# Last group of the third expert stage: which weights lie outside the ring of slots, an up matrix loaded in halves, and the order of two roots in the closing norm

## What is computed

```
def _hier_moe(h, wg, bg, we, be, w_gate, w_up, w_down):    # h (256, 1024)
    g_sel = argmax(h @ wg + bg)                            # 1 of 4 groups
    top_v, top_i = top_k(e_logits of that group, 2)        # 2 of its 8 experts
    ...
    y = (silu(x @ w_gate[e]) * (x @ w_up[e])) @ w_down[e]  # 1024 -> 512 -> 1024
    return sum over the two experts of weight * y

h = h + moe(_rmsnorm(h, norm2_w))
return _rmsnorm(h, final_norm_w)                           # the closing norm
```

## Time and profile before

| | |
|---|---|
| time, median of 3 runs | 1181.17 us (1181.11 to 1182.44) |
| the profiled execution | 1182.97 us, its span 1181.2 us |
| TensorE busy | 1083.0 us (92%) |
| VectorE, ScalarE busy | 333.1 us (28%), 227.3 us (19%) |
| DMA | 364.10 MB, mean 308 GB/s |
| the chain that ended last | TensorE 65%, DMA 27%, VectorE 4% |

### The profile page before, as it was taken

One profiled execution on the slowest core, in us unless ns is written; L12 is line 12 of the kernel. 1 busy time (PEld: TensorE's weight loads), 2 busy tenths in 40 slices (PEclk: granted clock), 3 DMA queues, 4 the chain that ended last, 5 costly groups with the idle time before them and its releaser, 6 DMA issues.

```text
span 1181.2 us, 15578 instructions
## 1 busy us (share of the span) xinstructions
PE 1083.0 (92%) x6382; PEld 539.8 (46%) x6382; DVE 333.1 (28%) x995; ACT 227.3 (19%) x517; POOL 1.0 (0%) x6
## 2 busy tenths in 40 slices
PE   9999999999999999999999989987877887779895
PEld 5555455554787545554465545422421242224231
DVE  1576463113013446111422656100100010001002
ACT  2145341111024423111122232100100010001001
POOL 0000000000000000000000000000000000000000
PEclk9999999999999999999999999999998998999998
DMA  9886368999433148999553248999999999999994
GB/s 318 182 228 242 131 226 358 422 417 379 147 131 143 72 174 319 421 422 341 183 193 143 80 178 322 411 427 428 429 426 428 428 428 427 428 429 428 426 417 197
DMA packets 82820, 364.10 MB, mean 308 GB/s; under 512 B 22690, under 2 KB 28100, under 8 KB 59076
## 3 DMA queue, kind: packets, MB, share of 16 engines
q1 hardware_dynamic: 81956, 363.04, 78.0%
q10 hardware_dynamic: 800, 0.17, 0.1%
HBM read 362.14 MB, written 1.05 MB: 307 GB/s over the span
## 4 chain that ended last, share of the span: by engine, by line
PE 65%; DMA 27%; DVE 4%; ACT 1%; issue 1%; SPq 1%; DVEq 0%
DMA weights<-in_expert_w_down_dram 16%; PE bank L1361 11%; PE bank L926 8%; PE bank L948 7%; DMA weights<-in_expert_w_up_dram 6%; PE bank L1463 5%; PE bank L1420 4%; PE bank L913 4%; DMA weights<-in_moe_w_up_dram 3%; PE bank L938 2%; PE bank L1405 2%; PE bank L1558 2%; PE bank L901 2%; DMA weights<-in_expert_w_gate_dram 2%; PE bank L890 2%; PE bank L1303 1%
## 5 line engine op out<-in xcount | busy, mean ns | idle before, releaser
L1361 PE MATMUL bank<-weights,projected 128*32 128x512 f32 (+1 forms) x1536 | 295.5, 540 | 38.4 <-DMA weights<-in_expert_w_gate_dram 23.7
L1361 PEld LDWEIGHTS bank<-weights,projected 128*32 128x32 f32 (+1 forms) x1536 | 101.9, 121 | 218.2 <-issue 171.4
L926 PE MATMUL bank<-weights,x_transposed 128*128 128x512 f32 x256 | 117.2, 600 | 0.0
L948 PE MATMUL bank<-weights,mixed 128*128 128x512 f32 x192 | 89.7, 604 | 1.6 <-DVE mixed L2578 1.0
L1420 PE MATMUL bank<-weights,work 128*32 128x512 f32 x432 | 53.1, 625 | 22.5 <-DMA weights<-in_expert_w_down_dram 18.0
L926 PEld LDWEIGHTS bank<-weights,x_transposed 128*128 128x128 f32 x256 | 46.4, 191 | 49.3 <-issue 48.4
L1463 PE MATMUL bank<-weights,projected 128*32 128x256 f32 x1024 | 62.2, 396 | 4.5 <-DMA weights<-in_moe_w_up_dram 4.5
L2080 ACT ACTIVATE work<-bank 128x512 f32<-128x512 f32 (+1 forms) x32 | 19.0, 594 | 223.2 <-PE bank L1420 183.2
L2845 DVE TENSOR_TENSOR work<-work,bank 64x512 f32<-64x512 f32 (+1 forms) x22 | 15.0, 682 | 161.3 <-PE bank L1361 159.6
L1558 PE MATMUL bank<-work,heads_transposed 128*128 128x512 f32 x120 | 55.8, 605 | 4.2 <-ACT work L2080 4.2
L2753 DVE COPY work<-bank 64x512 f32<-64x512 f32 (+1 forms) x30 | 20.7, 690 | 113.6 <-PE bank L1420 71.7
(11 more groups left out here) (380 smaller groups left out, 1167.4 us busy)
## 6 DMA issues: line engine op xcount, KB each, us to landing
weights<-in_expert_w_gate_dram SPq DMA_DIRECT2D x30, 2048.0 KB, 17.3
weights<-in_expert_w_up_dram SPq DMA_DIRECT2D x30, 2048.0 KB, 19.5
weights<-in_expert_w_down_dram SPq DMA_DIRECT2D x22, 2048.0 KB, 20.6
weights<-in_moe_w_gate_dram SPq DMA_DIRECT2D x16, 2048.0 KB, 13.0
weights<-in_moe_w_up_dram SPq DMA_DIRECT2D x16, 2048.0 KB, 15.6
weights<-in_moe_w_down_dram SPq DMA_DIRECT2D x12, 2048.0 KB, 13.5
weights<-in_sb_w_in_dram SPq DMA_DIRECT2D x6, 2048.0 KB, 14.6
weights<-in_w_in_dram SPq DMA_DIRECT2D x6, 2048.0 KB, 11.8
```

The lines of the kernel that those rows point to most:

```text
L926: i = mm(BANK[6 + t][:, :], XT[:, kt, t * P:(t + 1) * P], w[:, kt, :], start=kt == 0, stop=kt == KT - 1)
L948: i = mm(BANK[bank][:, :], mixT[:, kt, t * P:(t + 1) * P], w[:, kt, :], start=kt == 0, stop=kt == KT - 1)
L1361: i = mm(b[n_slots * c:n_slots * (c + 1), e * F:(e + 1) * F], x[:, kt, q * n_slots:(q + 1) * n_slots], w[c][:, col:col + F], start=kt == 0 ...
```

## The change

Three things. First, the four outside chunks are now gate0 and up0 of the last group instead of down0 and down1 (`EXTRA_AT = (0, 2)`, `EXTRA_KINDS`); `hidden` reads them with `extra_weights`, and down0 and down1 become ordinary ring blocks. The ring loads of the last group are now: gate1, up1, down0, gate2, up2, down1, gate3, up3, half of down2, down3. Second, up3 is loaded as two halves of both chunks (`load_last_up`), and TensorE begins on it when the first halves are there. Third, in the closing norm ScalarE takes tile 0's root before the two squares of tile 1, and VectorE works out tile 1's mean square between the two halves of tile 0's scaling.

```diff
-EXTRA_AT = (8, 14)
+EXTRA_AT = (0, 2)
+EXTRA_KINDS = ("gate", "up")
...
+                def load_last_up(j):
+                    for h in range(2):
+                        for c in range(2):
+                            n = chunk_no(L, j + c, True)
+                            cols = slice(h * (SLOT // 2), (h + 1) * (SLOT // 2))
+                            if h == 0:
+                                sp.wait_ge(chunk_done, (G - 1) * per_group + (n - NSLOT + 1))
+                            sp.dma_start(slot(n)[:, cols], expert_source(L, "up", G * 2 * units - 2 + c)[:, cols]
+                                         ).then_inc(slot_loaded[n % NSLOT] if h else quarters_loaded[0], 16)
...
-                            sp.dma_start(part, expert_source(L, "down", (G - 1) * 2 * units + c)[:, at:at + cols]).then_inc(extra_loaded[c // 2], 16)
+                            sp.dma_start(part, expert_source(L, EXTRA_KINDS[c // 2], (G - 1) * 2 * units + c % 2)[:, at:at + cols]).then_inc(extra_loaded[c // 2], 16)
...
-                        if 2 * (j // 2) not in EXTRA_AT:
+                        if j == first_chunk(units, "up", units - 1):
+                            load_last_up(j)
+                        elif 2 * (j // 2) not in EXTRA_AT and j != first_chunk(units, "up", units - 1) + 1:
...
-                        w = load(kind, u)
+                        outside = extra and u == 0
+                        x0 = 2 * EXTRA_KINDS.index(kind)
+                        in_halves = extra and (kind, u) == ("up", units - 1)
+                        if in_halves:
+                            pe.wait_ge(quarters_loaded[0], 16 * 8)
+                            w = [slot(chunk_no(L, first_chunk(units, kind, u) + c, last)) for c in range(2)]
+                        elif outside:
+                            pe.wait_ge(extra_loaded[x0 // 2], 16 * sum(len(parts) for parts in EXTRA_PARTS[x0:x0 + 2]))
+                        else:
+                            w = load(kind, u)
...
+                                if in_halves and kt == KT // 2:
+                                    load(kind, u)
...
-                                           w[c][:, col:col + F], start=kt == 0, stop=kt == KT - 1)
-                                    if e == per_chunk - 1 and kt == KT - 1:
+                                           extra_weights(x0 + c, kt) if outside else w[c][:, col:col + F], start=kt == 0, stop=kt == KT - 1)
+                                    if outside and kt == KT - 1 and c:
+                                        i.then_inc(extra_psum, 1)
+                                    elif e == per_chunk - 1 and kt == KT - 1 and not outside:
...
             moe(2, 5)
+            rstd_from(6, (0,))
             act.wait_ge(acc_ready, 6)
             for half in range(2):
                 i = ac(YS[:, 0, half, :], BANK[6 + half][:, :], ACT.Square, accum_out=final_ms[:, half:half + 1])
             i.then_inc(square_ready, 1)
-            rstd_from(6)
+            rstd_from(6, (1,))
...
+                        if after_half and cols.start == 0:
+                            after_half()
...
-                if L == 2:
-                    for t in range(T):
-                        norms(t)
+                    def variance_1():
                         dve.wait_ge(square_ready, 1)
+                        link(tt(newton[:, 1:2], final_ms[:, 0:1], final_ms[:, 1:2], ALU.add))
+                        ts(veps[:, 1:2], newton[:, 1:2], 1.0 / D, RMS_EPS, ALU.mult, ALU.add).then_inc(var_ready, 1)
+
+                    norms(0, variance_1)
+                    norms(1)
```

More of the change, by code:

```diff
@@ L1378, in down @@
                     def down(u, a, half):
-                        outside = extra and u < 2
-                        x0 = 2 * u
                         if a == 0 and half == 0:
                             pe.wait_ge(hT_ready, g * units + (unit0 + u + 1))
-                            if outside:
-                                pe.wait_ge(extra_loaded[u], 16 * sum(len(parts) for parts in EXTRA_PARTS[x0:x0 + 2]))
-                            elif extra and u == SLICE_UNIT:
+                            if extra and u == SLICE_UNIT:
                                 pe.wait_ge(slices_loaded, 16 * 4)
@@ L1417, in down @@
                                         col = f * D + hh * CH
-                                        w = (extra_weights(x0 + c, col // CH) if outside else
-                                             slice_weights(c, col // CH) if sliced else slot(n + c)[:, col:col + CH])
+                                        w = slice_weights(c, col // CH) if sliced else slot(n + c)[:, col:col + CH]
                                         i = mm(BANK[2 + hh][r0:r0 + n_slots, :], hT[:, f, n_slots * c:n_slots * (c + 1)], w,
@@ L1423, in down @@
                                         i.then_inc(y_psum, 1)
-                            i.then_inc(extra_psum if outside else chunk_done, 1 if outside else 2)
+                            i.then_inc(chunk_done, 2)
                             return
@@ L2104, in group @@
                     for u in range(units):
-                        act.wait_ge(chunk_done, g * per_group + (chunk_no(L, first_chunk(units, "gate", u), last) + 2))
+                        if last and L == 2 and u == 0:
+                            act.wait_ge(extra_psum, 1)
+                        else:
+                            act.wait_ge(chunk_done, g * per_group + (chunk_no(L, first_chunk(units, "gate", u), last) + 2))
                         if u:
@@ L2743, in outputs @@
                 def outputs(g, pair, last=False, banks=DOWN_BANK):
-                    if L == 2 and last and pair < 2:
-                        dve.wait_ge(extra_psum, pair + 1)
-                    elif pair % (pairs // units) == pairs // units - 1:
+                    if pair % (pairs // units) == pairs // units - 1:
                         dve.wait_ge(chunk_done, g * per_group + (chunk_no(L, first_chunk(units, "down", pair * units // pairs), last) + 2))
@@ L2842, in group @@
                         dve.wait_ge(silu_done, g * units + (unit0 + u + 1))
-                        dve.wait_ge(chunk_done, g * per_group + (chunk_no(L, first_chunk(units, "up", u), last) + 2))
+                        if last and L == 2 and u == 0:
+                            dve.wait_ge(extra_psum, 2)
+                        else:
+                            dve.wait_ge(chunk_done, g * per_group + (chunk_no(L, first_chunk(units, "up", u), last) + 2))
                         tt(HB[0:rows, :], SG[0:rows, :], BANK[1][0:rows, :], ALU.mult).then_inc(h_ready, 1)
@@ L3047, in _ @@
             mixer_residual(2, N_2 + 7, 1.0, 5, "rms", 5)
-            moe(2, 5, lambda t: normalise(6, "rms", X, t, from_psum=True))
+            moe(2, 5, lambda t, after_half=None: normalise(6, "rms", X, t, from_psum=True, after_half=after_half))
 SMALL_TOTAL = 16 * (NMOE * (1 + G + 2) + 4 + 1 + 5)
```

21 lines of the change are left out of this document (10 added, 11 removed).

## The result

The changed kernel is slower: 1187.38 us median of 6 runs (1186.74 to 1188.06), the kernel before in 6 runs 1182.76 us (1181.11 to 1185.62). The ratio is 1.0042, interval 1.0031 to 1.0053: +5.0 us on 1182.76, between +3.7 and +6.3; the two medians are 4.6 us apart. A second set of runs later gave 1.0035 (1.0022 to 1.0049). The three runs that were known ahead of the change had their median at 1181.17; with more runs the kernel before lies at 1182.1 to 1182.8. All ratios compare fast runs alone, which leaves out one execution of the kernel before (1860.9 us), one of the kernel before with its fourth load held (2249.6 us) and one of the version with up0 and down0 outside and two matmuls added (2836.6 us).

What follows compares the result with a forecast made beforehand. The prediction took the weight stream (426 to 429 GB/s) to bound the third stage. Last group +4.5 us and norm -0.6 us made +3.9 on the median of 1181.17: 1185.1 us, range 1183.4 to 1187.2.

Steps and rivals of the forecast that it cites:

- steps 1 to 3: Last group's ring: gate1 frees its slot at 1103.9, the stream runs dry from 1099.4, the fourth place lands 7.4 us late.
- step 1: Last group up to up0's end: nothing moves, the ring's first three places land as before, up0 ends at 1096.82.
- The first chunk's 7.8 us: Fourth ring place, gate2: a 2 MB chunk issued into an idle queue lands 7.8 us later, at 1111.7.
- The 6.8 us: Same chunk by the skill's rule, 2.0 us fixed plus bytes at 436 GB/s: a sum 1.0 us smaller; not adopted.
- The size of the hole: Last group's weight stream: fourth place's chunk 0 lands at 1111.7 instead of 1104.3, 7.4 us late.
- The start-up: Load into an idle queue: 2.9 us, the 7.8 us to landing less 4.9 us for half a block.
- steps 4 and 5: Tail of last group: no second hole, 0.4 us taken back, last quarter lands at 1170.8, down3 ends at 1171.9.
- The norm: Closing norm: sharpening begins 0.95 us earlier, 0.35 us of small steps move between the halves; term -0.6 us.
- Rival D: Tail: the hole plus a lower clock on down3's last quarter and final scatter, up to 1.7 us more, 1186.8; 9%.
- A: Likeliest case, last group: the hole goes through to the end, 1185.1 us, bounds 1183.9 to 1186.7; 76%.
- the group's term: Last group: down3 ends at 1171.9 instead of 1167.44, term +4.5 us.
- Rival B: Last group's ring: no hole if the fourth place is issued by 1096.5; -3.1 us, 1178.1, faster; 7%.

Runs made afterwards that it cites:

- the repeat: The changed kernel, nothing altered, run and profiled once more against the kernel before: ratio 1.0035 (1.0022 to 1.0049).
- up3 whole: The changed kernel with up3 loaded and awaited whole instead of in halves: ratio to the kernel before 1.0038 (1.0026 to 1.0050).
- old norm: The changed kernel with the closing norm of before, both roots behind the squares: ratio to the kernel before 1.0042 (1.0027 to 1.0058).
- held load: The changed kernel with up0 and down0 outside the ring, gate2's load held until gate1 is used: ratio to the kernel before 1.0035.
- two matmuls added: The changed kernel with one matmul added ahead of the wait for down3's last quarter and one before the last scatter: ratio to the kernel before 1.0032.

## Why the prediction came out as it did

The forecast was slower by 3.9 us, at 1185.1 with a range up to 1187.2. The measured median, 1187.38, lies 0.2 us above the range; the difference was +5.0 us (3.7 to 6.3) and +4.1 in the repeat.

- **The ring (steps 1 to 3): right in its order, 2 us off in its times.** The third load at 1075.9, the next 25.8 us later, nothing moved in between, gate1 with no wait. The text had named a gate1 that starts before 1096 as a sign of being wrong, and it started at 1094.59 (1094.0 and 1094.3 in two more profiles): not by another order of work, but since gate0 started about 2 us earlier (1080.1) than in the profile of before (1082.07), so step 1's "nothing moves" doesn't hold from one execution to the next. The first chunk's 7.8 us from the earlier trace rows were 7.7, and 7.7 to 8.0 in the other kernels with a dry queue. The 6.8 us, an estimate by the rule of the Trainium skill ("DMA: Bandwidth & Descriptors", section "Anatomy of one DMA — SWDGE (gpsimd) path"), is not what this queue shows.
- **The size of the hole: 7.4 us forecast, 5.6 on the first chunk and 6.6 on the second and at the end measured.** Two terms were off, in opposite directions. The release came 2.8 us behind the third's landing, not 4.5. The kernel before had run the previous group's down2 at the lower clock in its profiled execution (4.99 us at 1059.35, granted clock 0.56 to 1062.5; 3.64 in the changed kernel, at 1058.74) and was 1.3 us later for it; that was free there and stands on the chain now. It holds in all six profiles with a release at gate1's end: 2.6 to 2.8 us from landing to issue where down2 took 3.64 us (changed, again, up3 whole), 3.8 to 4.1 where it took 5.0 to 5.1 (old norm, held load, two matmuls added). Of the other 0.4 us, 0.3 lie in TensorE's rows: from the start of gate0 to the end of gate1 it took 21.5 us, where the text had added up 21.8. The start-up, on the other hand, had been put at 2.9 us from a first chunk alone, and at the second chunk and the last quarter it is 3.9.
- **No second hole, and down3 behind the last quarter (steps 4 and 5): right.** Last quarter at 1169.88 (1170.8 forecast), eight matmuls in 1.06 us, +3.55 us at down3's end against +4.5. Of the 0.9 us, 0.5 are the third place's earlier landing and 0.8 the smaller hole, less the 0.4 us that step 4 took back for the quarters. Those didn't show: from down2's landing to the last quarter's it was 10.1 us before (1153.7 to 1163.8) and 10.2 behind a full queue (1159.7 to 1169.9).
- **The norm: right,** -0.65 us for -0.6.
- **Rival D, given 9%, took place in the first profile:** 1.63 us in the final scatter for "up to 1.7". It isn't a property of the change, as the repeat shows; by how many of the timed runs it was met can't be told from their times. Nor is 1.7 us the most that the lower clock costs: gate2 took 10.04 us for 7.06 in the profile with the norm of before (granted clock 0.50 from 1115 to 1118, 0.57 to 1121.5).
- **The step that failed is the base of the sum:** "on the median of 1181.17 the same +3.9 gives 1185.1". The three runs had a spread of 1.3 us and the profiled one stood 1.8 us above their median, and I took the median as fixed and gave it no part in the bounds. The same kernel measured 1182.76 over six runs, 1.6 us of the 2.3 by which the forecast was low; the other 0.7 lie in the +3.9, which measured +4.6 between the medians and is inside the interval of the difference. With 1182.76 as the base the same +3.9 gives 1186.7; with the profiled execution, the text's own 1186.9. The runs show that executions of the kernel before lie between 1179.0 and 1185.6 us.
- **The bounds were added up wrongly too.** A's upper bound is 1185.1 + 0.4 + 0.6 = 1186.1, not 1186.7, and D's 1.7 us on top of it would reach 1187.8. The range ended at 1187.2 and so left out a part of D that the text itself allowed.
- **That +3.9 came near is in part luck.** In the first profile the group's term was 0.95 us too large and the lower clock added 1.63 us that the sum had at nothing; together with the norm they make +4.5.
- **Rival B was right in kind, its turning point too late:** issued 3.2 us ahead of the landing the first chunk is in step, but 1.2 us are lost by the last quarter; 10 us ahead nothing is. Without a hole or with this small one the versions are 2.5 to 4.4 us faster than before; B's sum for the changed kernel was 3.1.

## What to carry to other kernels

Blocks kept outside a ring delay the ring's first release by the time that they take themselves: put outside what is used after the first ring block, not before it. With three blocks in the ring and 9.8 us a block, the first slot has to come free well ahead of the third block's landing: here 3.2 us ahead still cost some 1.2 us and 10 us ahead nothing (no run lies between), and behind the landing it cost the delay and about 4 us more. It takes the queue's timeline, the distance between two issues, to see it. And a median of three has an uncertainty of its own, which belongs into the range of a forecast as small as 0.3%.

## What was not expected of the hardware

- The lower clock comes and goes in the same program. Behind the same wait of 2.7 to 2.9 us the block gate2 took 7.06 us in one profile of the changed kernel and 8.76 in the other, and 10.04 with the norm of before; the final scatter took 5.30 and 3.67.
- The traffic of a chunk ends well before its landing is told: in the changed kernel 1097 to 1098 us moves 33 GB/s, the third place's last packets, and it lands at 1098.9. And when the stream starts again the second chunk lands 6.0 us behind the first (1109.3, 1115.3), not 4.9; in the held version it is also 6.0. Part of this can be read from the 16 completions by which each load is told as landed. Those of the third place's second chunk are spread over 3.2 us (1095.65 to 1098.86), so the traffic thins out before the landing (1096 to 1097 moves 148 GB/s), and a release just ahead of the landing comes too late to keep the stream full. Those of the fourth place's first chunk are spread over 1.2 us, those of its second over 2.2, and there the last one alone comes 1.05 us behind the one before it. In the kernel before with its fourth load held the spread is 0.8 us for four chunks, and the late completion comes at the first chunk of up2 (1136.14, 6.2 us behind the chunk before it). The runs don't show why one falls behind.
